# 160 extra TensorE matmuls behind the last panel of a fp32r transformer block, in sixteen tile and stream forms

## The reference

```python
# first block
h = x + gla_mixer(rmsnorm(x), w_in, w_gate_up, b_gate, o_norm, w_out)   # 4 heads, chunks of 64
a = relu(rmsnorm(h) @ w_up)                                            # 2048 -> 8192
h = h + (a * a) @ w_down                                                # 8192 -> 2048
x2 = rmsnorm(h, final_norm)
# second block
q, k, v, g_sb, x_lru, g_lru = split(rmsnorm(x2) @ w_in_2)               # 2048 -> 6144
y_sb  = stick_breaking_attention(norm(q), norm(k), v) * silu(g_sb)      # 8 heads of 128
y_lru = rg_lru(causal_conv(x_lru)) * silu(g_lru)                        # linear recurrence over the tokens
out = x2 + concat(y_sb, y_lru) @ w_out_2                                # 2048 -> 2048
```

## Time and profile before

| what | us |
|---|---|
| median of two runs | 1512.14 (1511.2 and 1513.09) |
| profiled execution, own time | 1513.35 |
| profiled execution, span | 1511.2 |
| TensorE busy | 1494.4 (99% of the span) |
| VectorE busy | 854.1 |
| ScalarE busy | 718.2 |

### The profile page before, as it was taken

One profiled execution on the slowest core, in us unless ns is written; L12 is line 12 of the kernel. 1 busy time (PEld: TensorE's weight loads), 2 busy tenths in 40 slices (PEclk: granted clock), 3 DMA queues, 4 the chain that ended last, 5 costly groups with the idle time before them and its releaser, 6 DMA issues. The chain is left out here.

```text
span 1511.2 us, 17699 instructions
## 1 busy us (share of the span) xinstructions
PE 1494.4 (99%) x7210; PEld 1252.9 (83%) x7210; DVE 854.1 (57%) x889; ACT 718.2 (48%) x856; POOL 30.8 (2%) x54
## 2 busy tenths in 40 slices
PE   7999999999999999999999999999999999999998
PEld 6778888888888888888888888888888888888886
DVE  5555445555556545655555655565666776555653
ACT  5443444445444433444344433444554564556532
POOL 3000000000000000000000000000000001000000
PEclk9999999999999999999999999999999999999999
DMA  8455465657666566665666556665555456555553
GB/s 268 138 155 165 140 196 180 187 174 246 186 182 188 191 193 195 184 191 194 196 184 194 187 194 192 193 185 190 185 185 177 153 179 205 157 154 155 193 193 127
DMA packets 144720, 277.00 MB, mean 183 GB/s; under 512 B 10800, under 2 KB 10912, under 8 KB 144512
## 3 DMA queue, kind: packets, MB, share of 16 engines
q1 hardware_dynamic: 143056, 271.75, 58.4%
q0 software_dynamic: 1040, 3.07, 0.6%
q10 hardware_dynamic: 544, 1.05, 0.2%
HBM read 273.74 MB, written 2.10 MB: 183 GB/s over the span
## 5 line engine op out<-in xcount | busy, mean ns | idle before, releaser
L1009 DVE TENSOR_TENSOR w_lo<-raw,w_hi 128x1024 fp32r<-128x1024 f32 x508 | 620.1, 1225 | 596.3 <-ACT w_hi L726 594.7
L726 ACT ACTIVATE w_hi<-raw 128x1024 fp32r<-128x1024 f32 x508 | 537.1, 1059 | 719.7 <-PE banks L433 504.5
L431 PE MATMUL banks<-w_hi,xa 128*128 128x512 f32 x764 | 306.7, 402 | 0.2 <-DVE w_lo L1009 0.2
L431 PE MATMUL banks<-w_hi,xb 128*128 128x512 f32 x768 | 300.7, 392 | 1.9 <-DVE w_lo L1009 1.9
L433 PE MATMUL banks<-w_hi,xb 128*128 128x512 f32 x768 | 299.8, 390 | 0.0
L432 PE MATMUL banks<-w_lo,xb 128*128 128x512 f32 x768 | 299.8, 390 | 0.0
L433 PE MATMUL banks<-w_hi,xa 128*128 128x512 f32 x764 | 298.7, 391 | 0.0
L432 PE MATMUL banks<-w_lo,xa 128*128 128x512 f32 x764 | 298.5, 391 | 0.0
L444 PE MATMUL banks<-xa,w_hi 128*128 128x512 f32 x1024 | 256.5, 393 | 0.0
L444 PEld LDWEIGHTS banks<-xa,w_hi 128*128 128x128 f32 x1024 | 184.6, 189 | 33.0
L431 PEld LDWEIGHTS banks<-w_hi,xb 128*128 128x128 f32 x768 | 144.5, 188 | 32.0 <-DVE w_lo L1009 2.4
(11 more groups left out here) (202 smaller groups left out, 604.0 us busy)
## 6 DMA issues: line engine op xcount, KB each, us to landing
raw<-in_mlp_w_up SPq DMA_DIRECT2D x128, 512.0 KB, 3.8
raw<-in_mlp_w_down SPq DMA_DIRECT2D x128, 512.0 KB, 4.8
raw<-in_gla_w_in SPq DMA_DIRECT2D x96, 512.0 KB, 3.8
raw<-in_w_in SPq DMA_DIRECT2D x96, 512.0 KB, 3.7
raw<-in_gla_w_out SPq DMA_DIRECT2D x32, 512.0 KB, 4.1
raw<-in_w_out SPq DMA_DIRECT2D x32, 512.0 KB, 4.8
result<-stage SPq DMA_DIRECT2D x8, 256.0 KB, 3.5
h<-in_x ACTq DMA_DIRECT2D x2, 512.0 KB, 6.6
```

Source lines behind the costliest of these rows:

```text
L431: pe.matmul(o, xh[:, kt, xs], w_hi[:, n % RING, k, :], start=kt == 0, stop=False)
L726: act.activation(w_hi[:, n % RING, :, :], raw[:, n % RING, :, :], ACT.Copy)\
L1009: dve.tensor_tensor(w_lo[:, n % RING, :, :], raw[:, n % RING, :, :], w_hi[:, n % RING, :, :].bitcast(F32), ALU.subtract).then_inc(lo_ready, 1)
```

## The change

TensorE's program gets five helper functions and calls them behind the last panel. Nothing else is touched, no wait and no semaphore is added, and nothing reads what the added matmuls write.

```diff
+            def narrow_tiles(m):
+                for i in range(10):
+                    pe.matmul(banks[0:m, 4 + i % 4, :], xb[:, i, 0, 0:m], w_hi[:, i % RING, 0, :], start=True,
+                              stop=True)
+            def strided_tiles():
+                for i in range(10):
+                    pe.matmul(banks[:, 4 + i % 4, :], xb[:, i, 0, 0:S:2], w_hi[:, i % RING, 0, :], start=True,
+                              stop=True)
+            def half_rows():
+                for i in range(10):
+                    pe.matmul(banks[:, 4 + i % 4, :], xb[0:64, i, 0, 0:P], w_hi[0:64, i % RING, 0, :], start=True,
+                              stop=True)
+            def short_stream(m):
+                for i in range(10):
+                    pe.matmul(banks[0:m, 4 + i % 4, 0:S], xb[:, i, 0, 0:m], w_hi[:, i % RING, 0, 0:S], start=True,
+                              stop=True)
+            def far_stream():
+                for i in range(10):
+                    pe.matmul(banks[:, 4 + i % 4, :], xb[:, i, 0, 0:P],
+                              xb[:, i + 2, :, :].rearrange("p a b -> p (a b)"), start=True, stop=True)
             for t in range(PANELS):
                 run(t)
+            for m in (128, 127, 126, 124, 120, 112, 96, 64, 32):
+                narrow_tiles(m)
+            strided_tiles()
+            half_rows()
+            far_stream()
+            for m in (128, 127, 112, 64):
+                short_stream(m)
```

## The result

| | before | with the 160 matmuls |
|---|---|---|
| median, us | 1512.14 (2 runs) | 1540.51 (2 runs, 1539.28 and 1541.73) |
| profiled execution: own time, span, us | 1513.35, 1511.2 | 1541.73, 1539.6 |

The ratio is 1.0188 with a 95% interval of 1.0167 to 1.021: 28.4 us more by the medians, 28.4 by the spans too. That lies on the near side of 2%, and the interval reaches over it.

What follows compares the result with a forecast made beforehand. TensorE, busy 1494.4 of 1511.2 us, was taken as the bound. Starting at 1506.53, 32.0 + 0.94 us of matmuls plus the closing barrier gave span 1540.1, 28.9 more; added to median 1512.14, 1541.0 us, range 1538.8 to 1545.0.

Steps and rivals of the forecast that it cites:

- the sum of the list: All 160 added matmuls behind the last panel: 32.0 us of steps plus 0.94 us for tile-form changes.
- The place and the cover: Added matmuls start at 1506.53 behind the last panel, move nothing earlier; the output's 4.7 us tail hides the first ones.
- an instruction ahead of 1506.5 that has moved: Stated sign of being wrong: anything before the added matmuls shifting in time; none was expected to move.
- The step of 0.227 at 512 columns: 120 added matmuls streaming 512 columns, 0.227 us each whatever the tile width, 27.2 us together.
- The sign that I had kept for the lower bound: Added narrow tiles: loads shrinking with columns might shorten steps, saving 0.25 us on 90 narrow tiles, 0.1 on short ones.
- 0.120 at 256 columns: 40 added matmuls streaming 256 columns, 0.120 us each, 4.8 us together; step taken from the MLP's second pass.
- Six changes of form, 0.94 us: Six changes of tile columns, rows or stride in the added list, each draining the array; bounds 0 to 1.3 us.
- The price that I read in the attention scores: Change of tile form there: 0.09 us plus its load, giving 0.13 into 64 columns, 0.11 into 32, 0.19 into 128.
- The barrier: Closing barrier at the kernel's end, behind the last added matmul: 0.4 us.
- partial tiles whose load isn't hidden: Rival: added tiles under 128 columns or rows expose their loads; 1549.9 us, chance 0.10; with drains 1560.7, chance 0.03.
- The clock: Rival: idle columns in the added 64- and 32-column tiles halve the granted clock; 1542.7 or 1544.4 us, chance 0.14.
- Narrow is cheaper: Rival: in the added list form changes are free and loads shrink with columns; 1.3 us less, 1539.7, chance 0.14.

Runs made afterwards that it cites:

- 18-matmul kernel: Kernel before plus only 18 full matmuls (128-column tiles, streams of 512) behind the last panel; 1511.61 us against 1511.64, ratio 0.9997.
- the group of 32x128: Forty tiles of 32 rows, 128 columns, one of six tile-shape groups added behind the last panel of the kernel before; clock fell at 1524.34 us, no total given.

## Why the prediction was right, and where it was not

The forecast was 1541.0 us, and 1540.51 was measured; the sum of the list was 32.98 us, and 32.7 was measured. The mechanism was right: work behind the last panel, priced by its steps, less the tail's cover. That the times agree to 0.5 us is partly luck: the changed kernel's two runs lie 2.45 us apart, and executions of the 18-matmul kernel 4.4. Term by term:

- **The place and the cover.** Right. The first added matmul came 0.23 us behind the last panel's last one, behind the panel no other engine moved, and 18 matmuls alone cost nothing. One of my signs of being wrong did appear, an instruction ahead of 1506.5 that has moved: up to 1493 us nearly all of them had, by 1.9 us. It was a bad sign to choose, as executions differ there without the change (the 18-matmul kernel's last panel ended 3.65 us earlier), and the two shifts happened to cancel. Twice the list cost 32.4 us more by the time and 32.7 by the trace.
- **The step of 0.227 at 512 columns.** Right for 128 and 127 columns (2.26 and 2.27 us for ten). Too low by 1 to 6 ns for all narrower ones: the 90 took 1527.17 - 1506.49 = 20.68 us, and 90 x 0.227 is 20.43. The sign that I had kept for the lower bound, cheaper with fewer columns, was wrong at 512. Strided tiles took 0.233 each: 0.06 us more for the ten, where I had put nothing.
- **0.120 at 256 columns.** Right for 128 and 127. 112 columns took 0.118 and 64 columns 0.114, so here narrower was slightly cheaper. The forty took 4.7 us instead of 4.8.
- **Six changes of form, 0.94 us.** This is the term that failed, by its cause and its size. Four of the six are changes of columns, and they cost nothing. The two changes of rows cost 0.43 - 0.23 = 0.20 each (325 ns from the last strided start to the next load's start and 0.107 us for that load, 314 ns and 0.107 on the way back, where 0.23 would stand), 0.39 together; I had 0.38 for these two. The price that I read in the attention scores belongs to plain fp32 there. I had named that doubt as the lower bound, and it was the answer for the columns. The size of the price was nearly right: the wait was 0.10 to 0.11 us instead of 0.09, with the load behind it, and it came where the height changes (0.20, 0.15 and 0.12 us for 128, 64 and 32 columns, where I had 0.19, 0.13 and 0.11).
- **The barrier.** 0.24 us behind the last matmul instead of 0.4.

So -0.55 from the changes of columns, -0.1 from the short streams, +0.25 and +0.06 from the longer steps, and +0.05 from the groups of 64 rows and of xb, whose steps began a few ns above 0.227, make 0.3 less in the list, and the barrier 0.16 less: 28.9 became 28.4. The errors were small and in part cancelled.

The rivals: partial tiles whose load isn't hidden, no group showed. The clock: it didn't fall in the added list, nor in 14 us of tiles of 32 columns in the experiment; but the rival's nature was right, as idle rows can bring it down. A list with forty tiles of 32 rows on end would have met it, as the group of 32x128 did after 5.2 us. "Narrow is cheaper" was right for the columns' seams and wrong for the steps.

The chance of 0.36 for slower by over 2% was honest about a line 1.3 us away: the measured interval, 1.0167 to 1.021, includes that line.

## What to carry to other kernels

Work appended to the engine that sets the end costs its own start-to-start steps, less what the output's tail covers; both can be read in the timeline of before to a few tenths of a microsecond, while single executions of this kernel differ by up to 4 us. A price read from a row holds for that row's dtype and kind of change: check what else differs before it is carried over. In fp32r, tiles with fewer columns save nothing at streams of 512, changes of tile height cost up to 0.2 us each, so tiles of one height belong together, and small tiles of different row positions next to each other run side by side.

## What was not expected of the hardware

- Under dense streams of 512 columns the granted clock went with the rows of the tile, and not with its columns or the cells in use: at 32 of 128 rows it fell to half after 3.6 to 5.3 us of dense matmuls, at 64 rows (9.3 us) and at 16 or 32 columns of full height (9.3 and 14 us) it stayed full. The Trainium skill ("TensorE: Matmul & The Clock Gate", "Why this matters for your kernels") advises to keep TensorE busy continuously; here a matmul stream without a gap was not enough.
- Alternating 128 and 64 rows, with a drain at each step, also brought the clock down to half after some 5.7 us, and made the step 0.72 us.
- Tiles of fewer than 127 columns have slightly longer and uneven steps at 512 columns (228 to 234 ns on average against 227), whatever their address. Why is open.
